# Loads around the step from the trunk into the first expert, and the order of the last rows' norm, in a one-core diffusion step

## The reference, cut to what matters

```
h = rmsnorm(x, norm1_w) * (1 + scale1) + shift1;  p = h @ w_in
o = gated linear attention (two directions);      s = spatial gating of u, v
x = x + gate1 * (concat(o, s) @ w_out)
h2 = rmsnorm(x, norm2_w) * (1 + scale2) + shift2
probs = softmax(h2 @ router_w);  gates, idx = top_k(probs.T, cap)   # 16 experts; cap 64 sample, 16 prompt
xe = h2[idx]                                                        # rows that an expert takes
h = silu(xe @ w1[e]) * (xe @ w3[e]);  ye = (h @ w2[e]) * gates      # w1, w3: 1024x2048, w2: 2048x1024
x = x + gate2 * scatter_add(ye);      y = rmsnorm(x, final_norm_w)  # y = x * rsqrt(mean(x*x) + EPS) * w
```

## Time and profile before

| | us |
|---|---|
| median of three runs | 1329.9 (1328.8 to 1332.2) |
| profiled execution | 1329.4 |
| its span, first to last instruction | 1327.6 |
| TensorE busy | 1313.1 |
| VectorE, ScalarE, GpSimd busy | 462.1, 172.9, 110.8 |
| granted TensorE clock, mean | 0.996 |

### The profile page before, as it was taken

One profiled execution on the slowest core, in us unless ns is written; L12 is line 12 of the kernel. 1 busy time (PEld: TensorE's weight loads), 2 busy tenths in 40 slices (PEclk: granted clock), 3 DMA queues, 4 the chain that ended last, 5 costly groups with the idle time before them and its releaser, 6 DMA issues.

```text
span 1327.6 us, 24422 instructions
## 1 busy us (share of the span) xinstructions
PE 1313.1 (99%) x10821; PEld 468.9 (35%) x10821; DVE 462.1 (35%) x846; ACT 172.9 (13%) x281; POOL 110.8 (8%) x120
## 2 busy tenths in 40 slices
PE   9999999999999999999999999999999999999997
PEld 3554545555333333333333333333333333333332
DVE  3189897875141322212121304031221212130405
ACT  3443624225000000000000000000000000000002
POOL 0300001101110101101010101010100101000000
PEclk8999999999999999999999999999999999999999
DMA  9734623346899999999999999999999999999996
GB/s 331 241 128 141 247 72 127 109 185 269 342 421 420 415 429 416 430 416 428 418 427 419 426 420 425 421 416 429 416 432 415 428 418 426 420 427 420 429 407 248
DMA packets 63309, 472.98 MB, mean 356 GB/s; under 512 B 5669, under 2 KB 15730, under 8 KB 38698
## 3 DMA queue, kind: packets, MB, share of 16 engines
q1 hardware_dynamic: 56144, 453.66, 82.5%
q0 software_dynamic: 6320, 18.45, 4.6%
q10 hardware_dynamic: 810, 0.37, 0.1%
HBM read 459.08 MB, written 13.37 MB: 356 GB/s over the span
## 4 chain that ended last, share of the span: by engine, by line
PE 91%; DMA 5%; DVE 1%; another core or an unknown queue 1%; issue 1%; ACT 0%; SPq 0%; POOLq 0%; POOL 0%; DVEq 0%
PE psum L1341 47%; PE psum L1357 16%; PE psum L1368 8%; PE psum L893 8%; PE psum L1184 5%; DMA ring<-in_exp_w_dram 3%; PE psum L935 2%; PE psum L1123 2%; DMA ring<-in_ada_w_dram 1%; DMA ring<-in_w_in_dram 1%; PE psum L984 1%; PE psum L835 0%; PE psum L1087 0%; PE psum L1092 0%
## 5 line engine op out<-in xcount | busy, mean ns | idle before, releaser
L1341 PE MATMUL psum<-ring,both 128*32 128x512 f32 x6048 | 653.5, 592 | 1.5 <-DVE both L2222 0.8
L1341 PEld LDWEIGHTS psum<-ring,both 128*32 128x32 f32 x6048 | 197.1, 110 | 450.0 <-issue 447.0
L2279 DVE TENSOR_TENSOR both<-both,psum 128x512 f32<-128x512 f32 x48 | 50.9, 1061 | 551.2 <-PE psum L1341 551.2
L1357 PE MATMUL psum<-ring,both 128*32 128x512 f32 x2048 | 231.3, 592 | 0.0
L1700 ACT ACTIVATE both<-psum 128x512 f32<-128x512 f32 x48 | 28.7, 597 | 934.9 <-PE psum L1341 934.9
L1357 PEld LDWEIGHTS psum<-ring,both 128*32 128x32 f32 x2048 | 67.0, 110 | 152.8 <-issue 152.8
L1368 PE MATMUL psum<-ring,both 128*32 128x512 f32 x1024 | 118.7, 592 | 0.5 <-DMA ring<-in_exp_w_dram 0.4
L893 PE MATMUL psum<-ring,feat 128*128 128x512 f32 x240 | 104.0, 593 | 0.0
L744 POOL DMA_INDIRECT both<-xn_dram,both x45 | 49.4, 1099 | 576.2 <-DVE both L2290 566.8
L2309 DVE SCALAR_TENSOR_TENSOR both<-psum,both 64x512 f32<-64x512 f32 x32 | 24.0, 749 | 178.5 <-PE psum L1368 178.2
L1184 PE MATMUL psum<-ring,both 128*128 128x512 f32 x160 | 71.4, 596 | 0.0
(11 more groups left out here) (322 smaller groups left out, 638.4 us busy)
## 6 DMA issues: line engine op xcount, KB each, us to landing
ring<-in_exp_w_dram SPq DMA_DIRECT2D x190, 2048.0 KB, 19.2
ring<-in_ada_w_dram SPq DMA_DIRECT2D x8, 2048.0 KB, 7.8
ring<-in_w_in_dram SPq DMA_DIRECT2D x5, 2048.0 KB, 15.4
ring<-in_ada_w_dram SPq DMA_DIRECT2D x8, 1024.0 KB, 11.0
ring<-in_w_out_dram SPq DMA_DIRECT2D x2, 2048.0 KB, 7.9
acc_dram<-x POOLq DMA_DIRECT2D x5, 512.0 KB, 5.6
xn_dram<-feat POOLq DMA_DIRECT2D x5, 512.0 KB, 4.0
x<-acc_dram SPq DMA_DIRECT2D x5, 512.0 KB, 18.5
```

Of the source, the lines that this page charges most:

```text
L1341: mm = nc.tensor.matmul(role_bank(role)[f4 * PART:(f4 + 1) * PART, :], xe[:, kt, part * PART:(part + 1) * PART], w[:, kt % 2, f4 * 512:(f4 ...
L1357: mm = nc.tensor.matmul(role_bank("Y_A")[at:at + PART, :], h[:, c, part * PART:(part + 1) * PART], w[:, f, half * 512:(half + 1) * 512], s ...
L2279: role_stored(nc.vector.tensor_tensor(h_rows[:, part, :].rearrange("p (c a) -> p a c", a=PART), silu_h[:, part % 2, :].rearrange("p (a c) ...
```

## The change

Four edits.

1. In the trunk, TensorE turns `ws` behind the `zS` products and not ahead of `aS`. `job_numbers` lists it there too, so that the banks dealt in turn move: `aS` 6 to 5, `aP` 7 to 6, `zS` from 0, 1, 2, 3 to 7, 0, 1, 2, `wsT` 5 to 3.
2. Piece 5 of expert 0 waits for all five tiles of `xn2`, the prompt's too. The wait for `gathered_p` moves from piece 6 to piece 7.
3. `prompt_rows` stands behind the second half of piece 4, ahead of piece 5.
4. The end. SP waits for the last piece of weights before it stores the normed rows. For both kinds of last rows, VectorE multiplies by the norm weight while ScalarE squares; ScalarE takes the root of mean plus EPS in one step (scale and a bias column with EPS), VectorE the reciprocal of it; the last scaling is a product with one column, for the prompt rows on ScalarE, for the sample rows half on VectorE and half on ScalarE.

```
-    names += [("qkP",), ("wsT",)]
-    names += [("aS",), ("aP",)] + [("zS", h) for h in range(HEADS)] + [("zP",)]
+    names += [("qkP",)]
+    names += [("aS",), ("aP",)] + [("zS", h) for h in range(HEADS)] + [("wsT",), ("zP",)]
...
                 elif m == 5:
-                    sp.wait_ge(xn2_saved, 16 * ST)
+                    sp.wait_ge(xn2_saved, 16 * TILES)
...
-                if m == 6:
+                if m == 7:
                     sp.wait_ge(gathered_p, 16)
...
+            wait_expert_chunk(sp, EXPERT_LOADS - 1, LAST)
             for i, t in enumerate(OUT_ORDER):
                 sp.wait_ge(y_ready, i + 1)
...
-            pool.wait_ge(last_scaled, 1)
+            pool.wait_ge(last_scaled, 2)
...
-                              (0, 1, 1): [prompt_probs], (1, 1, 0): [all_slots], (2, 1, 0): [prompt_rows]}
+                              (0, 1, 1): [prompt_probs], (1, 1, 0): [all_slots], (2, 0, 1): [prompt_rows]}
...
             nc.scalar.activation(last_sq, last_rows, ACT.Square, accum_out=stats[:, 125:126]).then_inc(last_squared, 1)
-            act.wait_ge(last_recip, 1)
-            nc.scalar.activation(stats[:, 129:130], stats[:, 128:129], ACT.Sqrt).then_inc(last_rs, 1)
+            act.wait_ge(last_total, 1)
+            nc.scalar.activation(stats[:, 128:129], role_bank("R1_0")[:, 0:1], ACT.Sqrt, scale=1.0 / D, bias=eps_column).then_inc(last_root, 1)
+            act.wait_ge(last_weighted, 1)
+            act.wait_ge(last_rs, 1)
+            nc.scalar.activation(last_out[:, 256:512], last_out[:, 256:512], ACT.Copy, scale=stats[:, 129:130]).then_inc(last_scaled, 1)
...
                 nc.vector.tensor_tensor(last_rows, last_rows, last_out, ALU.add).then_inc(last_added, 1)
-                dve.wait_ge(last_total, 1)
-                mean_recip(stats[:, 128:129], role_bank("R1_0")[:, 0:1], D, last_recip, link_final)
+                dve.wait_ge(last_added, 1)
+                dve.wait_ge(final_half_loaded, 32)
+                nc.vector.tensor_tensor(last_out, last_rows, final_half, ALU.mult).then_inc(last_weighted, 1)
+                dve.wait_ge(last_root, 1)
+                nc.vector.reciprocal(stats[:, 129:130], stats[:, 128:129]).then_inc(last_rs, 1)
+                dve.wait_ge(last_weighted, 1)
                 dve.wait_ge(last_rs, 1)
-                dve.wait_ge(final_half_loaded, 32)
-                nc.vector.scalar_tensor_tensor(last_out, last_rows, stats[:, 129:130], final_half, ALU.mult, ALU.mult).then_inc(last_scaled, 1)
+                nc.vector.tensor_scalar(last_out[:, 0:256], last_out[:, 0:256], stats[:, 129:130], None, ALU.mult).then_inc(last_scaled, 1)
```

More of the change, by code:

```diff
@@ L322, in trunk_kernel @@
         final_w = both[:, 8192:9216]
+        eps_column = stats[:, 158:159]
         last_rows = both[:, 9216:9728]
@@ L397, in trunk_kernel @@
         last_p_squared = sem("last_p_squared")
-        last_p_recip = sem("last_p_recip")
+        last_p_root = sem("last_p_root")
         last_p_rs = sem("last_p_rs")
@@ L402, in trunk_kernel @@
         last_squared = sem("last_squared")
-        last_recip = sem("last_recip")
+        last_root = sem("last_root")
+        last_p_weighted = sem("last_p_weighted")
+        last_weighted = sem("last_weighted")
+        eps_ready = sem("eps_ready")
         last_rs = sem("last_rs")
@@ L986, in _ @@
             filled(mm, n)
-            pe.wait_ge(ws_loaded, 16)
-            n = JOB["wsT",]
-            wait_bank_free(pe, n)
-            for gr in range(GROUPS):
-                mm = nc.tensor.transpose(bank(n)[:, gr * P:(gr + 1) * P], ws[:, gr, :], ident)
-            filled(mm, n)
             pe.wait_ge(wa_loaded, 16 * 9)
@@ L1018, in _ @@
                         filled(mm, n)
+            pe.wait_ge(ws_loaded, 16)
+            n = JOB["wsT",]
+            wait_bank_free(pe, n)
+            for gr in range(GROUPS):
+                mm = nc.tensor.transpose(bank(n)[:, gr * P:(gr + 1) * P], ws[:, gr, :], ident)
+            filled(mm, n)
             wait_stored(pe, JOB["aP",])
@@ L2232, in scale_tiles @@
             def scale_tiles():
+                nc.vector.memset(eps_column, EPS).then_inc(eps_ready, 1)
                 dve.wait_ge(y_squared, TILES)
@@ L2245, in finish_prompt_rows @@
                 nc.vector.tensor_tensor(last_rows_p, last_rows_p, last_y_p[0:CAP_P], ALU.add).then_inc(last_p_added, 1)
-                dve.wait_ge(last_p_squared, 1)
-                mean_recip(stats[0:CAP_P, 147:148], stats[0:CAP_P, 145:146], D, last_p_recip, link_final)
-                dve.wait_ge(last_p_rs, 1)
-                nc.vector.scalar_tensor_tensor(last_rows_p, last_rows_p, stats[0:CAP_P, 148:149], final_w[0:CAP_P], ALU.mult, ALU.mult)\
-                    .then_inc(last_p_scaled, 1)
+                dve.wait_ge(last_p_added, 1)
+                nc.vector.tensor_tensor(last_y_p[0:CAP_P], last_rows_p, final_w[0:CAP_P], ALU.mult).then_inc(last_p_weighted, 1)
+                dve.wait_ge(last_p_root, 1)
+                nc.vector.reciprocal(stats[0:CAP_P, 148:149], stats[0:CAP_P, 147:148]).then_inc(last_p_rs, 1)
             def finish_sample_rows():
```

8 lines of the change are left out of this document (6 added, 2 removed).

## The result

The changed kernel took 1333.2 us, median of 20 executions (1329.6 to 1336.0), against 1328.9 (1327.6 to 1332.2, 20 executions) for the kernel before: ratio 1.0027, interval 1.0020 to 1.0034, so 3.6 us more. The prediction was 1328.0, within 1326.4 to 1331.0.

What follows compares the result with a forecast made beforehand. Bound: TensorE's chain from expert to expert, with DMA equally busy. Trunk 0, way in -0.1, last pieces -0.88, `Y_A` start -0.48, last scaling -0.42 sum to -1.9 us from a median of 1329.9: 1328.0, range 1326.4 to 1331.0.

Steps and rivals of the forecast that it cites:

- (a): Way into expert 1: without piece 5 beside it, the prompt's `xn2` store lands at 337.7, between 336.7 and 338.5.
- (b): Way into expert 1: piece 5, issued when the store lands, takes 7.8 us; with gathers beside it 346.4 (345.2 to 347.5).
- (c): Way into expert 1: prompt's gather issued at 339.85 when slots are there, takes 4 us, to 343.9 (343.0 to 346).
- (d): TensorE turns the rows by 345.45, waits for piece 5 until 346.4, begins the third part at 349.9, now 350.00.
- (e): Piece 6 follows piece 5 within 0.5 us, so the stream of weights runs about 2.5 us ahead.
- (f): The end: waits for the last two pieces of weights go with the stream's lead, -0.88 us, 0 as other end.
- (g): The end: VectorE is free sooner, so the `Y_A` product starts 0.07 us after TensorE, -0.48 us.
- (h): The end: from TensorE's sum to the last scaling 1.0 us where it was 1.42, -0.42 us (-0.25 to -0.55).
- rival A: Way in: the store lands by 336.7, piece 5 by 345.4, giving -0.9 instead of -0.1; 1327.2 us, chance 0.12.
- B: The end: the stream's lead does not last and the 0.88 us of waits stay; 1328.9 us, chance 0.13.
- D: The tail's steps wait for something else, so (g) and (h) give nothing; 1328.9 us, chance 0.07.
- C: Way in: store lands at 342.9 as now, piece 5 at 350.7, third part 4.2 us later; 1332.3 us, chance 0.08.

Runs made afterwards that it cites:

- e4: The kernel before with the trunk's edit alone (transposes of `ws` moved): 1328.7 us, ratio 0.9991.
- e3: The kernel before with only piece 5 held for the prompt's store; piece 6 and the turn of the rows as before: 1331.5 us, ratio 1.0015.
- e2: The kernel before with the way in alone (piece 5 held, piece 6 freed, rows turned sooner), trunk and end as before: 1334.4 us, ratio 1.0028.
- e5: The kernel before with piece 6 no longer held for the prompt's gather, piece 5 sent as before: 1333.6 us, ratio 1.0030.
- e7: The changed kernel with piece 5 sent as before, not held for the prompt's store: 1335.2 us, ratio 1.0038 to the kernel before.
- e8: The changed kernel with seven unread products ahead of TensorE's wait for the prompt's gather: 1333.7 us, ratio 1.0031 to the kernel before.
- e10: The changed kernel with three unread products ahead of TensorE's wait for the prompt's gather: 1330.6 us, ratio 1.0008 to the kernel before.
- e13: e10 with half of each row of piece 5 (8 KB of all 128) sent behind piece 3: 1331.4 us, ratio 1.0007.
- e14: The changed kernel with half of each row of piece 5 behind piece 3, piece 6 held for the gather again, no added products: 1330.5 us, ratio 0.9997.
- e6: The kernel before with the prompt's rows turned one half piece sooner, nothing else: 1329.9 us, ratio 1.0004.
- e1: The changed kernel without its way in (piece 5, the gather's hold and the turn as before): 1328.3 us, ratio 0.9988 to the kernel before.
- e12: e10 with half of the rows of piece 5 (64) sent behind piece 3: 1336.2 us, ratio 1.0048.
- e11: e1 with the turn of the prompt's rows one quarter of piece 5 sooner: 1329.2 us, ratio 0.9999.

## Why the prediction was wrong

Its steps, with the changed kernel's times less 2.55:

- **Trunk edit, 0:** right. e4 shows nothing that can be told from 0.
- **(a) store at 337.7 (336.7 to 338.5):** GpSimd's next work shows only the slots as releaser; the store lands 9.7 us after its issue, at 339.1. The direction was right (13.5 before), the size 1.4 us off, beyond my end. Two terms were mis-sized. I let piece 3 land at 336.74 as before; it landed 1.28 us later, by its slower last packets (0.94 for 0.62 us), which were not in any row that I had looked for. And I took all 2.10 MB of piece 5 off what moved from 336 to 343, but part of it had moved sooner, beside piece 3. The DMA view of before for this stretch gives the weights' queue only 1.61 MB, and GpSimd's 0.98 and not 0.51, which is 2.3 us at 434 GB/s and not 1.2:

```profile
q1 hardware_dynamic: 115, 1.61, 53.6%
q0 software_dynamic: 270, 0.98, 34.7%
```

- **(b) piece 5 lands 8.7 us after its issue, at 346.4:** issued at 339.1. When TensorE comes to it, at 349.4, it is there. In e3 it took 8.4 us, so the size was right and the issue 1.4 us late.
- **(c) gather issued at 339.85, 4 us:** this is the step that failed. It went out at 341.85: 1.2 us for the slots, which wait behind piece 3, and 0.75 us of issue behind them (the chain's row at 343.65), which I left out. Then it took 6.48 us for 4. Rows landed at 348.4, not 343.9, and past the 346 of my upper end. I took 3.15 us for a gather on quiet engines, which was 2.70, and added a little. e2, e5, e7, e8, e10 and e13 have 6.3 to 6.8 us beside the full stream, e3 6.0 beside piece 5 alone, e14 5.2 beside half a piece, e6 2.7 on quiet engines.
- **(d) third part at 349.9 (349.83 by its own terms):** at 354.33. Of the 4.43 us, the rows' lateness is 4.48, less the 1.52 us that lay idle in my sum (0.57 ahead of the turn and 0.95 for piece 5), plus 1.5 for the clock. The prediction said that "no term changes" with the clock; a new wait changed it. With e10's three products those 1.5 us went. The wait that I priced, up to 1 us for piece 5, did not arise.
- **(e) lead:** it came. The median landing fell from 19.2 to 14.1 us, more than the 2.5. But I counted only the gain of freeing piece 6; e5 shows that this line alone costs as much as the whole change, by the gather in (c).
- **(f) -0.88:** -0.92, a match that is in part luck. With the lead the waits for the last pieces are gone, in all profiles that have it. But e1, e4 and e6, with the old loads, have only 0.04 to 0.13 us of them too: the 0.88 was read from one execution, and is not what the lead is worth in most of the profiles.
- **(g) -0.48:** VectorE starts 0.08 us after TensorE's end and did 0.55 after: -0.47. **(h) -0.42:** 1.10 us for 1.42, -0.32, as ScalarE's half took 0.51 and not 0.45. The sum's products took 0.49 in this execution and 0.35 before. The end gave -1.62 in all, of -1.78, against this one execution of before. **(i) 0:** right, the prompt's scatter was released by ScalarE's scaling.

**The rule weighed**, from the Trainium skill's "DMA: Bandwidth & Descriptors", section "Queues, rings and completion order", has an engine drain many descriptors of a queue before it switches, so that the store would land by 336.7. It landed at 339.1, and before, in 2.5 us, q0 moved 0.23 MB, 56 packets of 4 KB, beside the 55 of 16 KB of q1: as many of the one as of the other, over all 16 engines. The views don't show the order within one engine, but a store that passed in one turn isn't in them. The rule doesn't show here, and rival A falls with it.

**Rivals.** A (piece 5 in time) and B (the lead doesn't last) fall; D falls at (g) and (h). C came nearest, with 1332.3 against 1333.2, but by another road: the store was sped up, and no wait for piece 5 arose. What took its place was the wait for the rows, the one that I held to be solved. That pair, a longer gather and a clock that falls behind the wait, was no rival of mine, though the gather stood in (c) with an end of 346; that end should have had its rival.

## What to carry to other kernels

A small gather that others wait for has to be costed by what runs beside it: 2.7 us on quiet queues and 6.5 us beside a stream of 2 MB pieces, here. A hold that looks like idle DMA time may be what keeps it short, so ask what a hold protects before it is moved. Price a new wait of TensorE with the slower products behind it, not by its length alone. And a wait read from one profile may be that execution's: the 0.9 us at the end were not there in three kernels with the same loads.

## What the runs showed of the hardware

- Nine kernels had a wait of 1.46 us or more around the rows' turn; in seven of them the granted clock fell to its lower level, 1.2 GHz, behind it, at a cost of 1.5 to 2.3 us in six (32 products in 5.1 to 5.9 us for 3.6) and of 3.0 us in e5. The waits don't sort by length: 1.46 us brought it down, 1.51 and 1.82 did not. With three products of 0.7 us in the gap and 0.18 or 0.88 us of idle time behind them it stayed up (e10, e13), with 4.25 us behind them it fell (e12).
- The last packets of piece 3 take 0.94 us in place of 0.62 when nothing stands behind it in its queue, and it lands as late with one packet behind; with four packets of 16 KB or eight of 8 KB behind they take 0.65 and 0.68. Piece 5 of the kernel before has nothing behind it either, and is not slowed. Its DMA view from 338.5 to 341 has 45 packets in 0.69 x 16 x 2.5 = 27.6 us, 0.61 us each:

```profile
q1 hardware_dynamic: 57, 0.74, 69.0%
```

So this is no general rule, and its cause is open.
- A load into 64 rows in place of 128 takes 0.98 us a packet of 16 KB, also beside the store, and slows the gather to 9.1 us.
- Executions come with two forms of the first 20 us. In the profile of before and in those of ten experiments the prompt's `xn2` store is issued at 328.4 to 329.7, in those of the changed kernel, e7, e11, e12 and e13 at 331.1 to 332.4. The longer form has the higher mean granted clock, and there the record and the products' times don't agree. Four products of 128x512 take 3.70 us in both kernels (at 11.29 before, at 14.57 changed). Before, the granted clock reads 0.56 and 0.50 in that stretch; in the changed kernel it reads 1.00.
